# Near attention of the second block: scaling on ScalarE, a weighing and the adaLN units moved, weight splits issued earlier

## The reference, cut to what matters

```python
def even_mixer(h, h_ctx, w_in, w_out, rpb, lb, hg_norm_w, with_ctx_out):
    ...
    a_lat = neighbourhood_attention(nh(na_q), nh(na_k), nh(na_v), nh(cna_k), nh(cna_v), rpb)
    g_lat, g_ctx = hgrn2_mixer(hg_q, (hg_ff, hg_fb), hg_i, hg_g, ...)
    y = jnp.concatenate([a_lat.reshape(b, s, NA_WIDTH), g_lat], axis=-1) @ w_out

def _hg_readout(o, g, norm_w):
    o = o * lax.rsqrt(jnp.mean(o * o, axis=-1, keepdims=True) + EPS)
    o = o * norm_w.astype(jnp.float32).reshape(HG_HEADS, 1, HG_VAL_DIM)
    return (o * jax.nn.silu(g.astype(jnp.float32))).astype(g.dtype)

# second_block, layer 0
mod = silu_c @ ada_w[layer] + ada_b[layer]          # adaLN, 6 * 1024 columns
x = x + gate_m[:, None, :] * y
h = modulate(rms_norm_2(x, norm_ffn_w[layer]), shift_f, scale_f)
x = x + gate_f[:, None, :] * conv_ffn(h, ...)
```

## Time and profile before

| | us |
|---|---|
| median of 3 runs | 1071.91 (1070.92 to 1072.86) |
| profiled execution | 1072.09 |
| its span | 1069.5 |
| near attention, first scores to first `evoA` product | 499.86 to 552.34 |
| `evoA` to the first feed-forward pair | 552.34 to 571.18 |

### The profile page before, as it was taken

One profiled execution on the slowest core, in us unless ns is written; L12 is line 12 of the kernel. 1 busy time (PEld: TensorE's weight loads), 2 busy tenths in 40 slices (PEclk: granted clock), 3 DMA queues, 4 the chain that ended last, 5 costly groups with the idle time before them and its releaser, 6 DMA issues.

```text
span 1069.5 us, 21436 instructions
## 1 busy us (share of the span) xinstructions
PE 1047.1 (98%) x9044; PEld 999.7 (93%) x9044; DVE 780.1 (73%) x1128; ACT 580.8 (54%) x883; POOL 66.7 (6%) x78
## 2 busy tenths in 40 slices
PE   8999999999999999999999999999999999999997
PEld 8989889999999999897688999999999999999996
DVE  6367778765576768987877999977687769677642
ACT  5456665565445675534656655533554457565432
POOL 2000000000010514000101000000010020000000
PEclk9999999999999999999999999999999999999999
DMA  9557656565755684444557888767768766555621
GB/s 283 175 182 255 223 172 213 181 198 181 243 169 161 190 224 157 132 145 157 200 183 251 275 288 274 268 250 290 261 224 284 227 213 208 187 182 179 236 79 40
DMA packets 165916, 220.29 MB, mean 206 GB/s; under 512 B 4498, under 2 KB 146222, under 8 KB 165821
## 3 DMA queue, kind: packets, MB, share of 16 engines
q1 hardware_dynamic: 164442, 215.67, 61.3%
q0 software_dynamic: 832, 1.65, 0.8%
q10 hardware_dynamic: 546, 1.60, 0.4%
HBM read 217.80 MB, written 1.11 MB: 205 GB/s over the span
## 4 chain that ended last, share of the span: by engine, by line
PE 78%; DVE 15%; ACT 3%; issue 2%; DMA 1%; SPq 0%; DVEq 0%; ACTq 0%
PE psG L577 19%; PE psG L579 18%; PE psG L578 18%; DVE wlo L1841 5%; PE psS L577 4%; PE psS L579 4%; PE psS L578 4%; DVE arow L1905 1%; PE psG L698 1%; PE psG L700 1%; DVE sq L2295 1%; PE psG L711 1%; DVE stat L2343 1%; PE psS L856 1%; PE psG L725 1%
## 5 line engine op out<-in xcount | busy, mean ns | idle before, releaser
L1841 DVE TENSOR_TENSOR wlo<-raw,whi 128x1024 fp32r<-128x1024 f32 x311 | 376.7, 1248 | 102.0 <-ACT whi L1252 96.7
L577 PE MATMUL psG<-Hlo,whi 128*128 128x256 f32 x1420 | 404.6, 285 | 2.5 <-DVE wlo L1841 1.4
L579 PE MATMUL psG<-Hhi,whi 128*128 128x256 f32 x1420 | 400.1, 282 | 0.0
L578 PE MATMUL psG<-Hhi,wlo 128*128 128x256 f32 x1420 | 399.9, 282 | 0.0
L1252 ACT CAST whi<-raw 128x1024 fp32r<-128x1024 f32 x311 | 314.2, 1047 | 117.5 <-PE psG L579 30.5
L577 PEld LDWEIGHTS psG<-Hlo,whi 128*128 128x128 f32 x1420 | 268.3, 189 | 6.4 <-issue 4.1
L578 PEld LDWEIGHTS psG<-Hhi,wlo 128*128 128x128 f32 x1420 | 268.4, 189 | 0.0
L579 PEld LDWEIGHTS psG<-Hhi,whi 128*128 128x128 f32 x1420 | 268.4, 189 | 0.0
L577 PE MATMUL psS<-Glo,whi 128*128 128x256 f32 x316 | 89.8, 284 | 0.0
L579 PE MATMUL psS<-Ghi,whi 128*128 128x256 f32 x316 | 89.1, 282 | 0.0
L578 PE MATMUL psS<-Ghi,wlo 128*128 128x256 f32 x316 | 89.1, 282 | 0.0
(11 more groups left out here) (452 smaller groups left out, 1780.8 us busy)
## 6 DMA issues: line engine op xcount, KB each, us to landing
raw<-in_ada_w_dram SPq DMA_DIRECT2D x48, 1024.0 KB, 5.6
raw<-in_ffn_w_up_dram SPq DMA_DIRECT2D x44, 1024.0 KB, 5.3
raw<-in_w_in_dram SPq DMA_DIRECT2D x29, 1024.0 KB, 6.5
raw<-in_ev_w_in_dram SPq DMA_DIRECT2D x26, 1024.0 KB, 5.5
raw<-in_ffn_w_down_dram SPq DMA_DIRECT2D x22, 1024.0 KB, 4.9
raw<-in_od_w_in_dram SPq DMA_DIRECT2D x12, 1024.0 KB, 8.1
raw<-in_w_in_dram SPq DMA_DIRECT2D x9, 512.0 KB, 6.7
raw<-in_w_o_dram SPq DMA_DIRECT2D x4, 1024.0 KB, 5.2
```

The costliest lines, as they stand in the source:

```text
L577: mm(o, a_hi, b_lo, start=first, stop=False, skip_group_check=shared)
L578: mm(o, a_lo, b_hi, start=False, stop=False, skip_group_check=shared)
L579: return mm(o, a_hi, b_hi, start=False, stop=last, skip_group_check=shared)
L1841: V.tensor_tensor(ring_half(wlo, v, h - H0[v]), src, ring_half(whi, v, h - H0[v]).bitcast(F32), ALU.subtract).then_inc(lo_split, 1)
```

## The change

`scale_output` goes from VectorE (one operation) to ScalarE (eight, one for each head and token half), at step 1 ahead of the exponentials. `na_weigh(0)` goes from the end of step 3 to step 4 behind `na_scores(4)`. The four units of adaLN part 4 are used one place earlier and one unit of part 11 goes from `na8b` to `na4b`. The split of `evoB0` moves from step 4 to step 3 on both engines. Those of `evoB1` to `evoB3` stay in steps 5 to 7, but on ScalarE ahead of the exponentials and on VectorE (steps 5 and 7) ahead of the normalisation. The splitting into `Hhi` and `Hlo` leaves `keep_na` and comes behind. The splits of `evoA0` and `evoA1` are made at step 8, of `evoA2` at step 9, of `evoA3` at step 10 (VectorE) or at the start of the `evoA` loop (ScalarE), and the loop then splits one half of the feed-forward pair at a time.

```diff
-              4: ("na2a", "na3a", "na4a", "na4b"), 7: ("up0.9", "up0.10", "fd0.0", "fd0.2"),
+              4: ("na1b", "na2a", "na3a", "na4a"), 7: ("up0.9", "up0.10", "fd0.0", "fd0.2"),
...
-              9: ("od0", "od1", "od2", "od3"), 11: ("na8b", "na9a", "tail2a", "tail2b")}
+              9: ("od0", "od1", "od2", "od3"), 11: ("na4b", "na9a", "tail2a", "tail2b")}
@@ TensorE
                 if s < NA:
                     na_scores(s)
+                if s == 4:
+                    na_weigh(0)
...
-                if s >= 3:
+                if s >= 4:
                     na_weigh(s - 3)
@@ ScalarE
+            def scale_output():
+                act.wait_ge(sub_inv, 2)
+                o = ot.rearrange("p t j v -> p (t j) v")
+                for n in range(8):
+                    ins = nc.scalar.activation(o[:, n, :], o[:, n, :], ACT.Copy, scale=lbc[:, 2, n:n + 1])
+                ins.then_inc(hg_gated, 1)
...
-                if s == 4:
-                    ahead(SPAN["hg"][1])
...
                     nc.scalar.copy(Hhi[:, 4:6, :], lg[:, 0, 0:2, :])
+                    ahead(SPAN["hg"][1])
...
+                if s == 1:
+                    scale_output()
+                elif s in (5, 6, 7):
+                    ahead(SPAN["evoB"][s - 5])
                 if s < NA:
                     exps(NG + s, [(pn_set(s)[:, i, :], psS[:, 2 * (s % 2) + i, :]) for i in range(2)], False)
+                if s >= NA:
+                    split_through(SPAN["evoA"][1 + s - NA])
                 if s in EVO_AT:
-                    ahead(SPAN["evoB"][EVO_AT[s]])
                     keep_turned(s - 2, 1)
...
-                if n in (1, 2):
-                    split_through(SPAN["fa0.0"][0], (2, 1)[n - 1])
-                else:
-                    ahead(u)
+                split_through(SPAN["fv0.0"][0], 1 if n else 2)
@@ VectorE
             for s in range(NA + 4):
+                j = (s - 5) // 2
+                kept_now = s >= 5 and s % 2 == 1
...
-                if s >= 5 and s % 2 == 1:
-                    keep_na((s - 5) // 2)
-                if s - 1 in EVO_AT:
+                if s == NA + 1:
+                    add_gated(SPAN["evoB"][3], 3, 0, 2, ready=False)
+                if kept_now:
+                    keep_na(j)
+                if s - 1 in EVO_AT and s <= NA:
                     add_gated(SPAN["evoB"][EVO_AT[s - 1]], EVO_AT[s - 1], 0, 2, ready=False)
+                if s in (5, 7):
+                    ahead(SPAN["evoB"][s - 5])
                 if 1 <= s <= NA:
                     normalise_near(s - 1)
-                if s == 1:
-                    scale_output()
-                elif s == 2:
+                if s == 2:
                     norm_output(0)
+                elif s == 3:
+                    ahead(SPAN["hg"][1])
                 elif s == 4:
-                    ahead(SPAN["hg"][1])
...
-                if s in EVO_AT:
-                    ahead(SPAN["evoB"][EVO_AT[s]])
+                elif s == 6:
+                    ahead(SPAN["evoB"][1])
+                if kept_now:
+                    split_na(j)
+                if NA <= s <= NA + 2:
+                    split_through(SPAN["evoA"][1 + s - NA])
             for n, u in enumerate(SPAN["evoA"]):
                 if n == 0:
-                    ahead(u)
+                    split_through(SPAN["fv0.0"][0], 1)
...
-                if n == 3:
-                    ahead(u)
-                elif n:
-                    split_through(SPAN["fa0.0"][0], (2, 1)[n - 1])
+                if n:
+                    split_through(SPAN["fv0.0"][0], 1)
```

More of the change, by code:

```diff
@@ L2208, in keep_na, with split_na @@
                 then(V.tensor_copy(vt[:, 1, :], psY[:, 0:S]), y_kept, NG + j + 1)
+            def split_na(j):
                 split_value(vt[:, 1, :], Hhi[:, j, :], Hlo[:, j, :], M_ready, 3 + j + 1)
@@ L2317, in _ @@
             keep_o(7)
[L2319 to L2324, removed]
             def norm_output(i):
```

## The result

The changed kernel takes 1074.07 us (median of 20 runs, 1070.20 to 1076.88), the kernel before 1071.92 (20 runs, 1070.92 to 1072.86). The ratio is 1.0019, 95% interval 1.0010 to 1.0027: 2.1 us slower, where 1.6 were forecast. One thing stands out before any row is read: the runs of the changed kernel lie 6.7 us apart, those of before 1.9.

A forecast was written before the change was run, and what follows sets the result against it. VectorE's order of work was taken to set the edited block. Start of `evoA` -0.8, new wait +3.6, squares -1.2 gave +1.6 us on 1071.9, so 1073.5 us; eight in ten from 1069.6 to 1075.9.

The forecast's parts named there:

- the new wait: TensorE before the last quarter of `evoA0`: stands 3.6 us, as VectorE awaits `evoA3`, landing after 4.7 us, before the last `keep_na`.
- the clock: Granted clock is 1.00 in both stretches of the old profile, so no clock term enters the sum.
- Late `evoB0`: Fifth 1 MB load ahead: landing 8.0 us after issue, ScalarE stands 2.9 us at step 3, TensorE's turn 1.7 late.
- Recurrence scaling: Step 1: VectorE loses 1.22 us, ScalarE gains 1.75 (1.05 to 2.5); step 3's bias starts about 0.35 us earlier.
- Fold and block end: VectorE in near attention: GpSimd's folds beside reductions save about 1.25 us; last normalisation ends 545.3, `evoA` starts 551.5.
- rival B: `evoA3` lands after 3.3 to 3.7 us: 1.0 to 1.4 us less, 1072.1 to 1072.5; chance 0.2.
- The squares: Block's tail: one weight cast instead of two on ScalarE ahead of the last squares, gain 1.2 us.
- C: Faster: `evoB0` not late, 1070.8; with rival B 1069.4; 1067.2 if the change does all it could; together chance 0.2.
- D: Slower: `evoB0` lands after 9.0 us, `evoA3` after 5.7, a fold meets a low part; 1075.5 to 1076.7, chance 0.15.

The follow-up runs named there:

- e3: Changed kernel with all adaLN units at their places of before the change: 1071.99 us, ratio 1.0004.
- e1: The changed kernel measured again, nothing edited: 1073.60 us, ratio 1.0020.
- e8: Changed kernel with last tile kept before `evoA3`'s low part, first `xT` update and adaLN sum before `fv0.0`'s, part 11's unit back at `na8b`: 1069.63 us, ratio 0.9982.
- e5: e8 with all adaLN places as before the change: 1069.94 us, ratio 0.9982.
- e4: e2 with the first `xT` update also ahead of the feed-forward's first low part: 1071.04 us, ratio 0.9993.
- e10: e8 with the low part of `evoA2` also behind the last `keep_na`: 1067.84 us, ratio 0.9961.
- e6: Changed kernel with 16 unused identity products on TensorE ahead of the last quarter of `evoA0`: 1072.96 us, ratio 1.0009.
- e2: Changed kernel with VectorE keeping and splitting the last tile before the low part of `evoA3`: 1073.21 us, ratio 1.0022.
- e6b: e6 with nine identity products instead of 16: 1072.58 us, ratio 1.0011.
- e9: e8 with `scale_output` on VectorE as before the change: 1068.51 us, ratio 0.9972.

## Why the prediction was right, and where it was not

**The total.** Forecast 1073.5, measured 1074.07; +1.6 and +2.1 us. That closeness is in good part luck: the sum put the new wait 1.4 us too high and left out a loss by the clock of about 2 us, and the two errors nearly cancel.

**Late `evoB0`: right.** 8.0 us after issue forecast, 8.3 measured; ScalarE's wait 2.9 forecast, 2.16 measured, because ScalarE itself came to it about 1 us later than forecast (`Hhi` cast ended at 514.73 - 0.37 = 514.4, not 513.4). The turn of step 4 came at 518.97 - 0.37 = 518.6, forecast 518.35. e3 takes the fifth load away and is 1.6 us under e1; e8 and e5, which differ from e4 by that load and by the place of the adaLN sum, have 0.9982 where e4 has 0.9993 (on another chip, with intervals that touch).

**Recurrence scaling: mis-sized.** The eight activations took 2.45 us, not 1.75: eight times the 0.31 of the row, so no overlap took anything off. I had both ends (1.05 and 2.5) and wrote that the order holds even at 2.5; it does not. The bias of step 3 was to be 0.35 us earlier and is 512.49 - 0.37 - 511.67 = 0.45 later. The sentence that does not hold is "TensorE turns the second half 0.9 us later, and VectorE, freed of 1.22 us, starts the bias of step 3 about 0.35 us earlier": the turn waited 1.53 us (510.68), and VectorE then stood 1.07 us for scores that TensorE makes behind that turn, so its freed 1.22 us were of no use to it. The Trainium skill's page "ScalarE: Activation LUTs", section "What ACT_TABLE_LOAD costs", gives 186 ns plus 0.833 ns an element, 93 ns more for a pointer operand and 93 less back to back; an estimate from it is 8 x 293 + 93 = 2440 ns, and the trace agrees with 2.45.

**Fold and block end: right.** The cast of `Hhi` is 0.29 again (1.04 before); the fold now falls beside a low part that took 1.46 against 1.23, so 0.23 us, not the up to 1.25 that the forecast had left open. The Trainium skill's page "SBUF — State Buffer", section "Who interferes with whom", has a VectorE instruction with two SBUF inputs contend with GpSimd; the trace agrees, with 1.46 against 1.23. The last normalisation ended at 545.50 - 0.37 = 545.1, forecast 545.3, and `evoA` began at 551.61 - 0.37 = 551.2, forecast 551.5.

**The new wait: right in place and releaser, 1.4 us too long.** 3.6 forecast (its own times, 553.7 and 557.2, give 3.5), 2.23 measured. The term is the landing of `evoA3`: 3.5 us, not 4.7. The middle of 3.7 and 5.7 was a wrong choice; of the forecast's own rows the one with a load right behind it was the nearest, and rival B had said so. With 3.5 in the sum the time would have been 1072.3. The trace agrees with the order in a ring that the Trainium skill's page "DMA: Bandwidth & Descriptors", section "Queues, rings and completion order", states: two loads of 1 MB were issued right behind `evoA3`, and it landed in 3.5 us all the same.

**The squares: right.** The wait is gone, 1.2 forecast. From the first `evoA` product to the pair it took 19.48 us against 18.84; less the hole of 2.23 that is 1.6 gained, 0.4 more than forecast, which I leave unassigned.

**What was missing: the clock.** "The granted clock is 1.00 in both, so no clock enters the sum" took the clock of the old trace for a property of the kernel. Of all the steps this one failed with the largest effect: the sum with the measured hole of 2.23 is +0.2 us, and the profiled execution, with no fall, has the same span as before (1069.4 and 1069.5). The rest is read from each run's mean granted clock. Six of the 20 of after:

| time us | span us | mean clock |
|---|---|---|
| 1070.20 | 1068.1 | 0.997 |
| 1071.25 | 1069.4 | 0.998 |
| 1074.09 | 1072.2 | 0.996 |
| 1074.94 | 1073.0 | 0.995 |
| 1076.17 | 1073.9 | 0.993 |
| 1076.88 | 1075.0 | 0.993 |

Each 0.001 of clock is 1.07 us of the span: from 0.998 to 0.993 is 5.3 us, and the spans in the table's second and last row differ by 5.6. The runs of before in the three tables of experiments all lie at 0.997 to 0.999, those of e10 too. The median of after's 20 is 0.996, 2.1 us, and that is about the difference between the medians. The table is the clear part of it. At 0.996 alone after has spans from 1070.2 to 1073.1; and when 1.07 us for each 0.001 under 0.998 are taken off all 20, an estimate, their median is 1069.2 us, no longer above the 1069.6 of before (first table), and they lie 4.0 us apart where they were 6.9. (That is coarse: the same step drives the spans of before from 1.4 to 2.9 us apart, since a mean clock also holds the last few us, where TensorE has no work left and the clock falls in every profile looked at, before, after and e10.) So the clock accounts for the difference of the medians and for part of the spread, as e6 says too. The rest of the spread stays open; the hole at the turn, which varied from 1.71 to 2.46 us with a load's landing, is a candidate, but how much of the spread it makes no run tests.

Where in the span the clock is lost was seen directly in e1, e2, e3, e6b and e8, each time at or behind a hole of 1.4 to 3.3 us in this block; in none of the 14 profiles does it fall anywhere else up to 1060 us. It was not seen in the longest runs of after, since none of them was the profiled one, so for those it is inferred. Nor does a profile without long holes promise a full clock: five of the 11 executions of e5 have 0.996, though its profiled one (0.998) has no hole over 1.13 us. That the change's order raises the median is shown by e10, which is 6.2 us lower. The profiles of the two, both at full clock in the block, differ by 3.2 us there (70.86 and 67.64); the other 3.0 are in what after's profiled execution does not show, the clock and the holes' variation, which no run parts.

**The rivals.** C (`evoB0` not late) fell with 8.3 us. B was right in its size of one landing, though its time was not. D did not come to pass by its mechanism. None of them had the clock in it.

## What to carry to other kernels

Before a wait for a load is moved ahead of anything, list what stands behind it on that engine and who reads that; keeping the tile first, then `xT` and the adaLN sum, then the low parts, together with the unit back at `na8b`, turned a loss of 2.1 us into a gain of 3.8. The order alone, in e4 and without the adaLN sum, got back to the time of before. A unit that is used earlier pushes another one into the ring ahead of later loads, so reprice the landing of each. And a hole of TensorE is not priced by its length alone: look at the granted clock behind it in more than one execution and at the spread of the runs, which here told of it before any trace did.

## What was not expected of the hardware

- The granted clock fell from 1.00 to 0.50 behind holes of 1.44, 1.92, 2.23, 2.29 and 3.27 us (e2, e8, e6b, e1, e3; in e3 already within it), for 3 to 7 us, and did not behind others of 1.53 to 2.46 us in after, e4 and e9 (1.79). The lower clock cost 1.7 us in four of these five, and 3.4 in e3.
- One product of the 128x128 identity with itself in f32 stands in the trace as two instructions and took 0.23 us, about twice what I had sized the fill by; such fill must be sized by its own row.
- Landing of a 512 KB load behind four and five 1 MB loads: 5.3 and 8.3 us. Behind four, but issued 0.9 us after the last of them and not some 4 us (e8): 9.3. With two 1 MB loads issued right behind it: 3.5.
